# Finishing the last expert job's prompt rows at their seats, with one indirect store over rows already stored

## The reference

```python
def hier_moe(h, w_router_group, w_router_expert, w_gate, w_up, w_down):
    ...
    g_val, g_idx = lax.top_k(pg, 1)
    ...
    e_val, e_idx = lax.top_k(jax.nn.softmax(le, axis=-1), TOP_K_EXPERTS)
    gate = g_val * (e_val / jnp.sum(e_val, axis=-1, keepdims=True))
    ...
    for e in range(N_EXPERTS):
        he = jax.nn.silu(x @ w_gate[e]) * (x @ w_up[e])
        y = y + dense_gate[:, e:e + 1] * (he @ w_down[e]).astype(jnp.float32)
```

## Time and profile before

| what | value |
|---|---|
| median of three runs | 727.58 us (723.72 to 727.69) |
| the profiled execution, its own time | 722.75 us |
| its span | 721.1 us |
| mean granted clock of TensorE in the span | 0.988 |
| TensorE (PE) busy | 689.0 us, 96% |
| VectorE (DVE) busy | 281.7 us, 39% |
| GpSimd (POOL) busy | 273.2 us, 38% |
| ScalarE (ACT) busy | 169.1 us, 23% |

### The profile page before, as it was taken

One profiled execution on the slowest core, in us unless ns is written; L12 is line 12 of the kernel. 1 busy time (PEld: TensorE's weight loads), 2 busy tenths in 40 slices (PEclk: granted clock), 3 DMA queues, 4 the chain that ended last, 5 costly groups with the idle time before them and its releaser, 6 DMA issues.

```text
span 721.1 us, 15001 instructions
## 1 busy us (share of the span) xinstructions
PE 689.0 (96%) x5740; PEld 345.0 (48%) x5740; DVE 281.7 (39%) x737; ACT 169.1 (23%) x358; POOL 273.2 (38%) x424
## 2 busy tenths in 40 slices
PE   6999999999979889998999999999999999999988
PEld 3555455874667556877555455333333332333322
DVE  1200036038668877877121165214202410430047
ACT  3100031137647563643022120001100100010100
POOL 2465246988488674873000003403400520200060
PEclk9999999999989999999999998999999999999999
DMA  9967605048940599989891165899999999999974
GB/s 296 272 173 246 191 11 116 10 146 225 229 118 3 157 299 311 303 265 268 303 426 77 58 249 197 300 387 399 410 413 423 420 421 408 425 425 411 404 264 146
DMA packets 88126, 191.18 MB, mean 265 GB/s; under 512 B 16486, under 2 KB 59894, under 8 KB 83565
## 3 DMA queue, kind: packets, MB, share of 16 engines
q1 hardware_dynamic: 70549, 150.10, 58.1%
...
## 4 chain that ended last, share of the span: by engine, by line
PE 58%; DVE 4%; DMA 1%; issue 1%; ACT 1%; POOL 0%; DVEq 0%; ACTq 0%; POOLq 0%
PE bank L1465 33%; PE bank L1359 8%; PE bank L1301 2%; PE bank L1577 1%; PE bank L1379 1%; PE bank L1204 1%; PE bank L1501 1%; PE bank L1350 1%; PE bank L1237 1%; PE bank L1207 1%; PE bank L1388 1%; DMA arena<-expert_rows,row_i 1%; DVE arena L2183 1%; DMA expert_rows<-proj 1%; PE bank L1196 1%
## 5 line engine op out<-in xcount | busy, mean ns | idle before, releaser
L1465 PE MATMUL bank<-arena,proj 128*32 128x512 f32 x1728 | 239.3, 600 | 0.8 <-issue 0.8
L1465 PEld LDWEIGHTS bank<-arena,proj 128*32 128x32 f32 x1728 | 67.0, 111 | 123.0 <-issue 122.5
L979 PE MATMUL bank<-arena,amT 128*128 128x454 f32 x256 | 102.0, 557 | 0.8 <-DVE amT L1855 0.8
L2649 POOL DMA_INDIRECT proj<-normed_rows,idx_of_quads x40 | 45.1, 1128 | 147.4 <-DVE proj L2410 129.3
L2547 POOL DMA_DIRECT2D arena<-in_cache_cmp_kv x128 | 68.6, 536 | 51.2 <-issue 43.4
L979 PEld LDWEIGHTS bank<-arena,amT 128*128 128x128 f32 x256 | 48.9, 194 | 49.7 <-issue 48.5
L1465 PE MATMUL bank<-amT,proj 128*32 128x512 f32 x288 | 70.1, 592 | 0.0
L2554 POOL DMA_DIRECT2D arena<-in_cache_slc_kv x96 | 56.8, 595 | 18.3 <-PE bank L996 6.3
L2419 DVE TENSOR_TENSOR proj<-proj,bank 128x512 f32<-128x512 f32 x12 | 8.3, 688 | 112.2 <-PE bank L1465 112.2
L2567 POOL COPY arena<-arena 128x268 f32<-128x268 f32 x64 | 37.8, 645 | 26.4 <-PE bank L976 18.8
L1465 PE MATMUL bank<-queries_and_bias,proj 128*32 128x512 f32 x288 | 42.7, 593 | 0.0
...
## 6 DMA issues: line engine op xcount, KB each, us to landing
...
arena<-in_cache_cmp_kv POOLq DMA_DIRECT2D x128, 64.0 KB, 2.5
arena<-in_cache_cmp_kv SPq DMA_DIRECT2D x128, 64.0 KB, 2.2
...
```

Of the source, the lines that this page charges most:

```text
L979: last = pe.matmul(ps(("in", c, i))[0:n, 0:WC], xnT[:, k, i * P:i * P + n], w_in[c % 2][:, k, :], start=k == 0, stop=k == KC - 1)
L1465: ins = pe.matmul(dst[part, :], rows[:, part], own if q < TRIO else shared, start=start, stop=stop)
L2649: po.indirect_dma_start(xg[j % 2][:, q * QD:(q + 1) * QD], None, scratch["n2"].rearrange("n (a c) -> (n a) c", a=QUADS), bass.IndirectOffs ...
```

## The change

The prompt rows that have a pick in job 11 are finished at their seats, and overwrite what was stored for them:

- A table by token (`by_token`: row of the other pick in `expert_rows`, its share, the root of the mean square, a zero) is computed by VectorE, written to memory by GpSimd ahead of job 6's gathers, and gathered by seat ahead of job 7's.
- Behind job 10's up product GpSimd gathers the normed rows of job 11's tokens again, by seat (`seat_rows`, 512 KB); ScalarE multiplies each by the root of its mean square, which gives the residual rows. The other pick's rows are gathered by seat with the last gathers (`other_rows`, 512 KB), and VectorE adds them times their share.
- A token with both picks in job 11 sits there twice: `same_token` is a 128x128 matrix with the share where two seats hold the same token. It is made from one product of ones by a diagonal of the tokens (in job 2's gate product). Two products of it by the halves of `ytok` give the sum for each seat. VectorE adds them to `seat_rows`, and GpSimd stores these over `y_prompt` with one indirect store, in which a seat without a prompt token has an index out of bounds and is left out.
- SyncE stores the four prompt tiles whole, each as soon as its gathered rows are added. The sample rows keep their one-hot matrix: two products, two additions, one store. Their gathered additions stand behind the two additions to `seat_rows` now.
- `WARM[4]` goes from 3 to 2.

The diff, its core:

```diff
-ROUTING = ("counts", "indices", "exponents", "quads", "last_shares", "places")
+ROUTING = ("counts", "indices", "exponents", "quads", "last_shares", "places", "seat_indices")
...
-WARM = (1, 1, 3, 3, 3)
-FINAL = (0, 1, 2, 3, 4, 7, 5)
+WARM = (1, 1, 3, 3, 2)
+FINAL = (0, 1, 2, 3)
+UNUSED = 1024
...
         last_hot = view(kTw, 300, 2, TILES)
         is_last = view(kTw, 310, 2, TILES)
-        last_token, last_share = view(kTw, 320, 1), view(kTw, 321, 1)
-        last_at = view(kTw, 322, TILES)
+        last_columns = view(kTw, 300, 2, 2 * TILES)
+        last_token, last_share, last_used = view(kTw, 320, 1), view(kTw, 321, 1), view(kTw, 322, 1)
+        last_at, last_shift = view(kTw, 323, 1), view(kTw, 324, 1)
+        not_last = view(kTw, 544, 2, TILES)
+        by_token = view(kTw, 554, TILES, 4)
...
+        seat_table = sb("seat_table", [P, 4])
+        seat_idx = sb("seat_idx", [P, 2], I32)
...
-        spot = blocks(pflat[:, 8704:8960], 2) + blocks(KCT[:, 0:2 * P], 2) + blocks(VC[:, 0, :], 1)
+        same_token, token_diagonal, spot_of_sample = pflat[:, 8704:8704 + P], pflat[:, 8704 + P:8960], VC[:, 0, 0:NS]
+        seat_rows, other_rows = (view(pflat, (2 + i) * D, D) for i in range(2))
...
+            for i in range(TILES - 1):
+                sp.wait_ge(y_ready, i + 1)
+                sp.dma_start(out["y_prompt"][0, i * P:(i + 1) * P, :], xh[:, i, :]).then_inc(st_res, 16)
+
...
-
-            for n in range(2 * TILES):
-                i, c = n % TILES, slice(n // TILES * 512, (n // TILES + 1) * 512)
-                sp.wait_ge(y_ready, n + 1)
-                dst = out["y_prompt"][0, i * P:(i + 1) * P, c] if i < 4 else out["y_sample"].rearrange("b q d -> (b q) d")[:, c]
-                sp.dma_start(dst, xh[0:ROWS[i], i, c]).then_inc(st_res, 16)
-            sp.wait_ge(st_res, 32 * TILES)
...
+            sp.wait_ge(y_ready, TILES + 3)
+            sp.dma_start(out["y_sample"].rearrange("b q d -> (b q) d"), xh[0:NS, TILES - 1, :]).then_inc(st_out, 16)
+            sp.wait_ge(st_res, 16 * (TILES - 1))
+            sp.wait_ge(st_out, 16 * (N_OUT + 1))
...
-                    pe.wait_ge(last_ready, 1)
+                    pe.wait_ge(last_ready, 3)
...
-                last = pe.matmul(BH[:, 0:1], picks[n], last_hot[:, n % 2, n // 2:n // 2 + 1], start=n == 0, stop=n == 2 * TILES - 1)
+                c = n % 2 * TILES + n // 2
+                last = pe.matmul(BH[:, 0:2], picks[n], last_columns[:, :, c], start=n == 0, stop=n == 2 * TILES - 1)
...
+                    if n == 2:
+                        pe.wait_ge(last_ready, 2)
+                        pe.matmul(BH[:, P:2 * P], ones, token_diagonal, start=True, stop=True).then_inc(last_full, 1)
...
+            def last_rows(stationary, rows, b, signal):
+
+                for half in range(2):
+                    pe.wait_ge(y_taken, 2 * NJ - 1 + half)
+                    pe.matmul(bank[FINAL[b + half]][0:rows, :], stationary, ytok[(NJ - 1) % 2][:, half * 512:(half + 1) * 512],
+                              start=True, stop=True).then_inc(signal, 1)
+
+            last_rows(same_token, P, 0, last_full)
+
...
-            pe.wait_ge(last_ready, TILES)
-            for n in range(2 * TILES):
-                i, half = n % TILES, n // TILES
-                if i == 0:
-
-                    pe.wait_ge(y_taken, 2 * NJ - 1 + half)
-                if n >= 7:
-                    pe.wait_ge(y_ready, n - 6)
-                pe.matmul(bank[FINAL[n % 7]][0:ROWS[i], :], spot[i][:, 0:ROWS[i]], ytok[(NJ - 1) % 2][:, half * 512:(half + 1) * 512],
-                          start=True, stop=True).then_inc(last_full, 1)
...
+            last_rows(spot_of_sample, NS, 2, last_full)
...
+                if (m, j) == (0, NJ - 1):
+                    sc.wait_ge(ld_seat, 48)
+                    sc.activation(seat_rows, seat_rows, ACT.Copy, scale=seat_table[:, 2:3]).then_inc(sg_ready, 1)
...
-                ve.wait_ge(sg_ready, j + 1)
+                ve.wait_ge(sg_ready, j + 1 + (j == NJ - 1))
...
-            def last_spread():
+            def last_seats():
 
                 ve.wait_ge(last_full, 1)
-                link(ve.tensor_copy(last_share, BH[:, 0:1]))
-                for i in range(TILES):
-                    ve.tensor_scalar(spot[i], table["row"], last_at[:, i:i + 1], last_share, ALU.is_equal, ALU.mult)\
-                        .then_inc(last_ready, 1)
+                ve.tensor_copy(last_share, BH[:, 0:1])
+                link(ve.tensor_copy(last_used, BH[:, 1:2]))
+                link(ve.scalar_tensor_tensor(last_shift, last_token, -float(UNUSED), last_used, ALU.add, ALU.mult))
+                link(ve.tensor_scalar(seat_idx[:, 0:1], last_shift, float(UNUSED), None, ALU.add))
+                ve.tensor_scalar(spot_of_sample, table["row"][:, 0:NS], last_at, last_share, ALU.is_equal, ALU.mult).then_inc(last_ready, 1)
+                ve.tensor_scalar(token_diagonal, ident, last_token, None, ALU.mult).then_inc(last_ready, 1)
+
+            def seats_of_same_token():
+
+                ve.wait_ge(last_full, 2)
+                ve.tensor_scalar(same_token, BH[:, P:2 * P], last_token, last_share, ALU.is_equal, ALU.mult).then_inc(last_ready, 1)
+
+            def seat_indices():
+
+                ve.wait_ge(ld_seat, 32)
+                ve.tensor_copy(seat_idx[:, 1:2], seat_table[:, 0:1]).then_inc(routed, 1)
...
+            def other_row_added():
+
+                ve.wait_ge(ld_seat, 64)
+                link(ve.scalar_tensor_tensor(seat_rows, other_rows, seat_table[:, 1:2], seat_rows, ALU.mult, ALU.add))
+
+            def last_half_added(x, rows, half):
+
+                part = x[:, half * 512:(half + 1) * 512]
+                return ve.tensor_tensor(part, rows[:, :], part, ALU.add)
...
+            link(ve.tensor_scalar(not_last, is_last, -1.0, 1.0, ALU.mult, ALU.add))
+            other = by_token[:, :, 0]
+            link(ve.tensor_tensor(other, over_f[:, 0], over_f[:, 1], ALU.subtract))
+            link(ve.tensor_tensor(other, other, not_last[:, 0], ALU.mult))
+            link(ve.tensor_tensor(other, other, over_f[:, 1], ALU.add))
+            link(ve.tensor_scalar(other, other, EARLY - 1.0, None, ALU.min))
+            ve.tensor_copy(by_token[:, :, 2], st[:, 16:16 + TILES])
+            ve.memset(by_token[:, :, 3], 0.0)
...
             link(ve.tensor_scalar(inside[:, :, :], over_f, 0.0, None, ALU.is_lt))
-            ve.sem_inc(routed, 1)
...
-            link(ve.tensor_scalar(is_last, is_last, -1.0, 1.0, ALU.mult, ALU.add))
-            link(ve.tensor_tensor(gates1[:, :, :], gates1[:, :, :], is_last, ALU.mult))
-            link(ve.tensor_scalar(last_at, table["tile"], -1.0, last_token, ALU.mult, ALU.add))
-
-            last_spread()
+            link(ve.tensor_tensor(gates1[:, :, :], gates1[:, :, :], not_last, ALU.mult))
+            link(ve.tensor_tensor(by_token[:, :, 1], gates1[:, 0, :], gates1[:, 1, :], ALU.add))
+            ve.sem_inc(routed, 1)
+            link(ve.tensor_scalar(last_at, table["tile"][:, TILES - 1:TILES], -1.0, last_token, ALU.mult, ALU.add))
+
+            last_seats()
...
+                if n == 2:
+                    seats_of_same_token()
...
-            for i in range(1, TILES):
+                if (m, j) == (2, NJ - 2 * TRIO):
+                    seat_indices()
+            ve.sem_inc(y_ready, 1)
+            for i in range(1, TILES - 1):
                 gathered_rows(i)
+                ve.sem_inc(y_ready, 1)
+            other_row_added()
+            for half in range(2):
+                ve.wait_ge(last_full, 3 + half)
+                last_half_added(seat_rows, bank[FINAL[half]], half).then_inc(y_ready, 1)
+            gathered_rows(TILES - 1)
             ve.sem_inc(early_added, 1)
...
-            for n in range(2 * TILES):
-                i, half = n % TILES, n // TILES
-                x = xh[0:ROWS[i], i, half * 512:(half + 1) * 512]
-                ve.wait_ge(last_full, n + 2)
-                ve.tensor_tensor(x, bank[FINAL[n % 7]][0:ROWS[i], :], x, ALU.add).then_inc(y_ready, 1)
...
+            for half in range(2):
+                ve.wait_ge(last_full, 5 + half)
+                last_half_added(xh[0:NS, TILES - 1, :], bank[FINAL[2 + half]][0:NS, :], half).then_inc(y_ready, 1)
...
+                if j == NJ // 2:
+                    po.wait_ge(routed, routed_at("places"))
+                    po.dma_start(scratch["by_token"].rearrange("(i p) c -> p i c", p=P), by_token).then_inc(ld_seat, 16)
+                if j == NJ // 2 + 1:
+                    po.wait_ge(ld_seat, 16)
+                    po.indirect_dma_start(seat_table[:, :], None, scratch["by_token"], bass.IndirectOffsetOnAxis(idx[:, NJ - 1:NJ], 0))\
+                        .then_inc(ld_seat, 16)
...
-            po.wait_ge(routed, routed_at("places"))
+            po.wait_ge(product, after(1, NJ - 2))
+            po.wait_ge(ld_seat, 32)
```

(13 more changed lines are left out.)

23 lines of the change are left out of this document (20 added, 3 removed).

## The result

The changed kernel took 727.83 us (median of 20 runs, 723.85 to 733.32), the kernel before 725.18 us on the same chip (20 runs). The ratio, taken over the fast runs, which leave out one of the kernel before at 745 us, is 1.0047, interval [1.0029, 1.0065]. By it the changed kernel is 3.4 us slower (2.1 to 4.7), where 2.3 us faster was forecast. The profiled execution has a span of 727.5 us at a mean granted clock of 0.976 (before 721.1 us, 0.988). The sign of the difference does not agree with the forecast. That the time of 727.8 us lies in the range is luck of the level: the range was built on a median of 727.58, 2.4 us above that of the 20 runs, and moved down by as much it would end at 727.1.

What follows compares the result with a forecast made beforehand. TensorE, busy 96%, was taken as the bound, with a chain of waits at the end. Terms -2.5 - 0.9 + 0.3 + 0.8 = -2.3 us, from a 727.58 us median to 725.3 us; range 719.0 to 729.5.

Steps and rivals of the forecast that it cites:

- The tail, -2.5 us: After job 11's down product: ten final products become four, VectorE's queue ends last, end at 718.6 instead of 721.1 us.
- the seventh addition: Tail, VectorE: adding the other pick's rows, same kind as the six 1.3 us additions for tiles 1 to 3, to 708.7.
- the branch gap: Tail: 0.72 us before VectorE's final additions, read as VectorE's branch and expected to be paid again.
- I take it as hidden: Tail: GpSimd's scatter, landing at 716.5, lets GpSimd end near 717.5, 1.1 us before the sample store.
- rival (1): Tail: the scatter ends the program, landing 6.8 us; tail -1.3 instead of -2.5, 726.5 us; chance 0.17.
- The start, -0.9 us: Start of the experts: one filler matmul fewer starts the shares' products some 1.6 us earlier; net -0.9 us.
- rival (3): Start of the experts: the clock stays down through the shares; +0.4 for that term, sum -1.0, 726.6 us; chance 0.16.
- The added product, +0.3: TensorE, between pieces of job 2's gate product: one more 128x128 product, +0.3 us, bounds 0.14 and 0.93.
- The last stored rows, +0.8: Job 10's last store: the 512 KB of seat rows inserted ahead delay it, +0.8 us, between +0 and +3.35.
- Rival (2): Job 10's last store falls back into full load, +3.35 us, plus 1.7 half clock; +1.95, 729.5 us; chance 0.12.
- The two small tables, 0: GpSimd before jobs 6 and 7: table by token and seat table delay nothing that is awaited, 0 us.

Runs made afterwards that it cites:

- both pairs: Profiles of the kernel before and the changed kernel, unchanged: the first two, then two more on a chip where the kernel before takes 724.66 us; +3.1 us each.
- run 4: Changed kernel with the scatter into a scratch tensor and no wait for the prompt stores; ratio to the kernel before 0.9986.
- run 1: Changed kernel with WARM[4] back at 3, three pieces of filler before the shares; ratio to the kernel before 0.9958.
- run 9: Changed kernel, unchanged, on a chip where the kernel before takes 731.05 us; ratio to the kernel before 0.9991.
- run 2: Changed kernel with GpSimd's wait for the scatter's landing behind the branch on crowding; ratio to the kernel before 0.9969.
- run 10: Changed kernel with three pieces of filler again and the wait for the scatter's landing behind the branch; ratio to the kernel before 0.9979.
- run 16: Changed kernel, unchanged, on a chip where the kernel before takes 724.66 us; ratio to the kernel before 1.0043.
- run 17: Changed kernel with three pieces of filler and the landing wait behind the branch, a second time; ratio 0.9980 to the kernel before at 732.37 us.
- run 7: Changed kernel with only a quarter of each seat row gathered (128 KB for 512); ratio to the kernel before 0.9992.
- run 11: Kernel before with one piece of filler less ahead of the shares; ratio to the unedited kernel before 1.0000.
- run 14: Changed kernel with job 11's hidden values ahead of tile 0's additions and the stored-row gathers held until job 11's up product; ratio to the kernel before 1.0126.
- run 3: Changed kernel with the seat rows gathered early, ahead of job 8's quarters, into their own area; ratio to the kernel before 1.0009.
- run 6: Kernel before plus the unused 512 KB gather of the seat rows behind job 10's up product; ratio to the unedited kernel before 1.0012.

## Why the prediction was wrong

By its steps, on the chips where the difference can be measured (the table above; both pairs agree within 0.4 us in every row):

- **The tail, -2.5 us: right as far as it went, measured -2.86 to the sample's store, then lost again, +2.6 to +2.75.** The four products, the seventh addition, the branch gap (0.70 for 0.72), the two additions of 64x512 (1.28 for 1.3) are all there, and the store is issued 7.22 us after the last result's first product for 10.08. The step that failed is "I take it as hidden". GpSimd was put at 9.2 us behind that product and ended at 12.5. Of the 3.3 us, 1.3 are the later issue of the scatter (4.69 us behind the product for 3.4: tile 3's store, put at "2.1 to 3 us", took 4.6 beside the gathers), -0.6 the landing (4.2 for 4.8), and 2.6 what GpSimd does behind the landing until the program ends: 3.6 us, for the 0.7 to 1.0 of the prediction. This last is the term that was mis-sized most.

  That is rival (1), at 11.5 in its own working; chance 0.17. It had the place right, but its own price came from a landing of 6.8, and not from the closing. The price of the wait for the stores is shown by no single edit: run 4 has 10.82 us, but runs 1 and 9 have 10.83 and 10.81 with the wait in place. With the wait for the landing behind the branch the stretch from the scatter's issue to the end is 6.4 to 6.6 us for 7.8 to 7.9 where the stores hold the scatter (runs 2 and 10; first profile and run 16), and 6.9 for 7.2 where they don't (run 17; runs 1, 7 and 9).

  The Trainium skill's page "DMA: Bandwidth & Descriptors" was weighed in the prediction with an estimate of 3.2 us for 512 KB. The scatter moved 0.25 MB and took 4.2; gathers of twice the bytes took 4.1 to 6.8, so the rows can't tell a dear receipt in memory from the rest of the cost. For the other page of the Trainium skill, "SBUF — State Buffer", "SBUF: two separate sides": the scatter's issue took 1.42 us beside VectorE's additions, for 0.95 as a rule, which agrees with it, at a price of 0.5 us.
- **The start, -0.9 us: measured +0.5 in the first pair; -0.6 in the second, then lost.** From the index copy to the end of job 0's second turns it is 15.98 us in both profiles of the kernel before, 16.51 in the changed kernel's first and 15.41 in run 16. In the first, the granted clock stayed at 0.50 through the shares. That is rival (3), chance 0.16, and its +0.4 for this term fits. It also occurred in runs 4, 11 and 14, and not in runs 2, 3 and 7 (2.36 to 2.52 us) and hardly in 9 and 16 (2.6), which have the same filler. The step that failed there is that the clock would be back 0.9 us into the shares. From there to the last store every piece of TensorE in that profile has the length that it had before, but for the added product. In run 16 the clock was back in time and 0.57 us was won, but TensorE waited 0.74 us ahead of job 9's down product and took 0.2 more around it. The step that failed there is the assumption behind the whole term, that TensorE alone paces the expert stage.
- **The added product, +0.3: its piece took 0.42, and the stretch of 320 matmuls around it grew by 0.56 (35.03 for 34.47).** So the copy to the last store grew by 0.5 + 0.6 = 1.1 us in the first pair and by -0.6 + 0.6 + 0.9 = 0.9 in the second, where the terms of that stretch (-0.9 and +0.3) came to -0.6.
- **The last stored rows, +0.8: measured +1.8 to +2.0.** The term was the right one and mis-sized. The seat rows' share is 0.7 to 1.4 us (run 6), near what was worked out from the bytes. Another 0.25 us goes with GpSimd's two added waits (landing to first gather 0.97 us for 0.73). Rival (2) had the place and the sign; the store took 6.45 and not 8.0, and its threshold of 3.1 us wasn't reached. The program became slower by four smaller terms together.
- **The two small tables, 0.** They were priced by what GpSimd delays with them, and not by what they take from the queues, which were full of weights. All profiles with them move 10 to 24 GB/s less from 500 to 540 us than all those without, an estimated 1.0 to 2.3 us. What of it reached the last store, as the rest of +1.9, and run 16's wait isn't shown.
- **Not in the sum: +0.45 us** between tile 0's additions and the down product. The turns of the hidden values took 1.12 us for 0.66, behind 4.3 us of idle TensorE for 2.6; the clock granted from 704 to 706 was 0.50. The prediction names this effect in rival (2) only.
- **The level.** 725.3 was made from a median of three runs; on 20 runs the kernel before is at 725.2, so -2.3 would have been 722.9.

In sum: (-0.9 + 0.3) became +1.0; +0.8 became +1.9; nothing became +0.5; -2.5 became -0.2. With -0.15 from the first gather to tile 0 that is +3.1 in place of -2.3.
